# One moving operand of 512 columns for the gate and up products of the FFN, with the correction rows in the other half of the bank

## The reference, cut to what matters

```python
def _conv_ffn(x, w_up, conv_w, conv_b, w_down):      # x (1,256,1024), w_up (1024, 2*2816), w_down (2816,1024)
    u = _causal_dwconv(x @ w_up, conv_w, conv_b)     # 3 taps along the tokens, per feature
    gate, up = jnp.split(u, 2, axis=-1)
    return (jax.nn.silu(gate) * up) @ w_down
```

## Time and profile before

| | us |
|---|---|
| median of 3 runs (lowest, highest) | 829.93 (829.03, 830.1) |
| profiled execution, its own time | 828.89 |
| its span in the profile | 827.1 |
| PE busy in the span | 767.7 (93%) |
| DVE busy | 487.9 (59%) |
| ACT busy | 376.3 (45%) |

### The profile page before, as it was taken

How to read it: one execution, slowest core, us unless ns; L and a number is a source line. 1 busy time by engine, 2 the same in 40 slices (tenths; PEclk the granted TensorE clock), 3 DMA queues, 4 the chain that set the end, 5 groups by cost and what they waited for, 6 DMA issues and landing times.

```text
span 827.1 us, 16238 instructions
## 1 busy us (share of the span) xinstructions
PE 767.7 (93%) x6690; PEld 647.9 (78%) x6690; DVE 487.9 (59%) x843; ACT 376.3 (45%) x573; POOL 49.2 (6%) x91
## 2 busy tenths in 40 slices
PE   6999999999999999999999999999999877677676
PEld 6999998999999998999998999899955443344343
DVE  4455567767676678867864255487775523323326
ACT  4556664545545556567454553474332211111124
POOL 0200032000000000110101000000001000000000
PEclk9999999999999999999999999999999979879889
DMA  8964453556556554444342233449989999999993
GB/s 281 315 210 131 145 162 106 181 175 203 167 188 202 172 185 153 160 147 154 102 154 59 98 103 103 146 159 367 420 327 419 421 421 419 422 420 421 421 420 138
DMA packets 89170, 194.34 MB, mean 235 GB/s; under 512 B 3646, under 2 KB 69537, under 8 KB 76689
## 3 DMA queue, kind: packets, MB, share of 16 engines
q1 hardware_dynamic: 86640, 186.66, 61.3%
q0 software_dynamic: 1888, 4.61, 1.8%
q10 hardware_dynamic: 576, 2.14, 0.7%
HBM read 192.35 MB, written 1.05 MB: 234 GB/s over the span
## 4 chain that ended last, share of the span: by engine, by line
PE 72%; DMA 17%; DVE 5%; ACT 2%; issue 1%; SPq 1%; ACTq 0%; DVEq 0%
DMA expert_w<-in_expert_w_up 17%; PE PG L2041 15%; PE PG L2043 14%; PE PG L2042 14%; PE PG L2646 3%; PE PM L2041 3%; PE PM L2043 3%; PE PM L2042 3%; PE PM L2676 1%; PE PM L2497 1%; ACT whi L844 1%; PE PG L2668 1%; SPq L676 1%; PE PM L2122 1%; DMA rows<-in_norm_mix 1%
## 5 line engine op out<-in xcount | busy, mean ns | idle before, releaser
L2041 PE MATMUL PG<-hT_hi,whi 128*128 128x256 f32 (+1 forms) x816 | 235.8, 289 | 0.0
L2043 PE MATMUL PG<-hT_hi,wlo 128*128 128x256 f32 (+1 forms) x816 | 230.6, 283 | 0.0
L2042 PE MATMUL PG<-hT_lo,whi 128*128 128x256 f32 (+1 forms) x816 | 230.5, 282 | 0.0
L1357 DVE TENSOR_TENSOR wlo<-raw,whi 128x2048 fp32r<-128x2048 f32 x73 | 167.2, 2291 | 65.8 <-ACT whi L844 65.7
L2041 PEld LDWEIGHTS PG<-hT_hi,whi 128*128 128x128 f32 x816 | 153.9, 189 | 6.1 <-issue 2.8
L2043 PEld LDWEIGHTS PG<-hT_hi,wlo 128*128 128x128 f32 x816 | 154.2, 189 | 0.0
L2042 PEld LDWEIGHTS PG<-hT_lo,whi 128*128 128x128 f32 x816 | 153.7, 188 | 0.2
L844 ACT ACTIVATE whi<-raw 128x2048 fp32r<-128x2048 f32 x73 | 139.4, 1910 | 21.4 <-PE PG L2043 19.1
L2646 PE MATMUL PG<-expert_w,xw 128*32 128x256 f32 x992 | 74.2, 449 | 36.8 <-DMA expert_w<-in_expert_w_up 36.8
L2646 PEld LDWEIGHTS PG<-expert_w,xw 128*32 128x32 f32 x992 | 36.7, 124 | 59.0 <-issue 47.3
L1952 DVE SCALAR_TENSOR_TENSOR y_lo<-PG,small,y_hi 128x512 fp32r<-128x512 f32 x16 | 12.0, 750 | 98.4 <-ACT y_hi L1276 98.4
(11 more groups left out here) (525 smaller groups left out, 1338.3 us busy)
## 6 DMA issues: line engine op xcount, KB each, us to landing
expert_w<-in_expert_w_gate SPq DMA_DIRECT2D x32, 1024.0 KB, 26.7
expert_w<-in_expert_w_up SPq DMA_DIRECT2D x32, 1024.0 KB, 26.8
expert_w<-in_expert_w_down SPq DMA_DIRECT2D x32, 1024.0 KB, 26.9
raw<-in_ffn_w_up SPq DMA_DIRECT2D x22, 1024.0 KB, 5.0
raw<-in_w_in SPq DMA_DIRECT2D x22, 1024.0 KB, 5.1
raw<-in_moba_w_qkv SPq DMA_DIRECT2D x12, 1024.0 KB, 6.9
raw<-in_ffn_w_down SPq DMA_DIRECT2D x11, 1024.0 KB, 4.9
raw<-in_moba_w_o SPq DMA_DIRECT2D x4, 1024.0 KB, 5.1
```

Source lines behind the costliest of these rows:

```text
L1357: dve.tensor_tensor(lo_of(n), raw[:, n % R, :], hi_of(n).bitcast(F32), ALU.subtract).then_inc(s_lo, 1)
L2041: pe.matmul(dst, lh, rh, start=start, stop=False, **kw)
L2042: pe.matmul(dst, lh, rl, start=False, stop=False, **kw)
L2043: return pe.matmul(dst, ll, rh, start=False, stop=stop, **kw)
```

## The change

The activations' hi and lo parts become the two halves of one tile `hT`, so that one matmul can stream 256 columns of hi and 256 columns of lo as one moving operand of 512 columns against the hi weights. Its result fills a whole PG bank: hi·hi in the first half, hi·lo in the second. The lo weights times the hi activations are added to the second half, the correction. A new function `halves` issues these two matmuls for every k-tile in the place of the three of `split3`, in the FFN's gate and up granules only. Both halves have to be added afterwards: ACT copies the correction half of two banks to SBUF (`correction`), DVE adds the first half to it (the new function `halves` of the vector program) into `gate_sum` and `up_sum`, and `affine` and `taps` read these sums. PE waits for the adds instead of the taps. The issue order of ACT and DVE changes as the diff shows.

```diff
-        hT_hi = place("hT_hi", [P, KD, NT], 29440, F32R)
-        hT_lo = place("hT_lo", [P, KD, NT], 38144, F32R)
+        hT = place("hT", [P, 2, KD, NT], 29440, F32R)
+        hT_hi, hT_lo = (hT[:, i, :, :] for i in range(2))
+        gate_sum, up_sum = (place(n, [P, 2, SEQ], PH + 98304 + 2048 * i) for i, n in enumerate(("gate_sum", "up_sum")))
@@ scalar
-            def affine(j, dst, bank, tile0, s_done, par, cnt, gran):
-                act.wait_ge(s_gran, gran)
+            def correction(n, j, dst, bank, s_done, it):
+                act.wait_ge(s_gran, n + 1 + 6 * it)
+                act.activation(dst[:, :, :], PG[:, bank:bank + 2, SEQ:2 * SEQ], ACT.Copy).then_inc(s_done, 1)
+
+            def affine(j, dst, src, tile0, s_sum, s_done, par):
+                act.wait_ge(s_sum, 4 * j + 1)
                 for f in range(2):
-                    act.activation(dst[:, par, f, :], PG[:, bank + f, 0:SEQ], ACT.Identity,
+                    act.activation(dst[:, par, f, :], src[:, f, :], ACT.Identity,
             def ffn_step(n, j, par, it, first=False, last=False):
-                affine(j, cgate, 0, 2 * j, s_gaff, par, None, n + 1 + 6 * it)
+                correction(n, j, gate_sum, 0, s_gaff, it)
                 hi_part(n + 2, it)
-                act.wait_ge(s_gtap, 3 * j + 3)
+                affine(j, cgate, gate_sum, 2 * j, s_gtap, s_gaff, par)
+                correction(n + 1, j, up_sum, 2, s_uaff, it)
+                hi_part(n + 3, it)
+                act.wait_ge(s_gtap, 4 * j + 4)
                 act.activation(cgate[:, par, :, :], cgate[:, par, :, :], ACT.Silu).then_inc(s_gsilu, 1)
-                if last:
-                    hi_part(n + 3, it)
-                affine(j, cup, 2, FT + 2 * j, s_uaff, par, None, n + 2 + 6 * it)
-                if not last:
-                    hi_part(n + 3, it)
-                else:
+                affine(j, cup, up_sum, FT + 2 * j, s_utap, s_uaff, par)
+                if not first:
                     hi_part(n + 4, it)
                 act.wait_ge(s_hid, j + 1)
                 act.activation(hid_hi[:, par, :, :], hid[:, par, :, :], ACT.Copy).then_inc(s_hidhi, 1)
-                if not first and not last:
-                    hi_part(n + 4, it)
@@ vector (taps reads src = gate_sum or up_sum; its waits count 3 and 4 per step)
+            def halves(j, dst, bank, s_aff, s_tap):
+                dve.wait_ge(s_aff, 3 * j + 1)
+                dve.tensor_tensor(dst[:, :, :], PG[:, bank:bank + 2, 0:SEQ], dst[:, :, :], ALU.add).then_inc(s_tap, 1)
             def ffn_step(n, j, par, it, first=False, last=False):
-                taps(cgate, par, 0, 2 * j, s_gaff, s_gtap, j)
+                halves(j, gate_sum, 0, s_gaff, s_gtap)
                 lo_part(n + 2, it)
-                if last:
-                    lo_part(n + 3, it)
-                taps(cup, par, 2, FT + 2 * j, s_uaff, s_utap, j)
-                if not last:
-                    lo_part(n + 3, it)
+                taps(cgate, gate_sum, par, 2 * j, s_gaff, s_gtap, j)
+                halves(j, up_sum, 2, s_uaff, s_utap)
+                lo_part(n + 3, it)
+                taps(cup, up_sum, par, FT + 2 * j, s_uaff, s_utap, j)
                 dve.wait_ge(s_gsilu, j + 1)
-                dve.wait_ge(s_utap, 3 * j + 3)
+                dve.wait_ge(s_utap, 4 * j + 4)
                 dve.tensor_tensor(hid[:, par, :, :], cgate[:, par, :, :], cup[:, par, :, :], ALU.mult).then_inc(s_hid, 1)
+                if not first:
+                    lo_part(n + 4, it)
                 dve.wait_ge(s_hidhi, j + 1)
                 dve.tensor_tensor(hid_lo[:, par, :, :], ...).then_inc(s_hidlo, 1)
-                if not first:
-                    lo_part(n + 4, it)
@@ tensor
+            def halves(n, bank, it=0, ready=None):
+                pe.wait_ge(s_lo, n + 1 + 6 * it)
+                hw, lw = w_of(n)
+                for f in range(2):
+                    for k in range(KD):
+                        if ready is not None and f == 0 and k % 4 == 0:
+                            pe.wait_ge(ready[0], ready[1 + k // 4])
+                        x = slice(P * f, P * f + P)
+                        pe.matmul(PG[:, bank + f, :].rearrange("p (i n) -> p i n", i=2), hw[:, k, x], hT[:, :, k, 0:SEQ],
+                                  start=k == 0, stop=False, skip_group_check=True)
+                        mm = pe.matmul(PG[:, bank + f, SEQ:2 * SEQ], lw[:, k, x], hT[:, 0, k, 0:SEQ], start=False, stop=k == KD - 1,
+                                       skip_group_check=True)
+                mm.then_inc(s_gran, 1)
             def ffn_step(n, j, par, it, first=False):
-                    pe.wait_ge(s_gtap, 3 * j)
+                    pe.wait_ge(s_gtap, 4 * j - 3)
-                features(n, 0, hT_hi, hT_lo, slice(0, SEQ), it, halves=(s_xlo, 7, 8) if first else None)
+                halves(n, 0, it, (s_xlo, 7, 8) if first else None)
-                    pe.wait_ge(s_utap, 3 * j)
-                features(n + 1, 2, hT_hi, hT_lo, slice(0, SEQ), it)
+                    pe.wait_ge(s_utap, 4 * j - 3)
+                halves(n + 1, 2, it)
```

More of the change, by code:

```diff
@@ L1466, in col, with taps @@
                 return cols[:, bass.ds(i, n)]
-            def taps(dst, par, bank, tile0, s_aff, s_tap, j):
+            def halves(j, dst, bank, s_aff, s_tap):
+                dve.wait_ge(s_aff, 3 * j + 1)
+                dve.tensor_tensor(dst[:, :, :], PG[:, bank:bank + 2, 0:SEQ], dst[:, :, :], ALU.add).then_inc(s_tap, 1)
+            def taps(dst, src, par, tile0, s_aff, s_tap, j):
                 for back in (1, 2):
@@ L1472, in taps @@
                         if back == 1:
-                            dve.wait_ge(s_aff, 2 * j + f + 1)
+                            dve.wait_ge(s_aff, 3 * j + f + 2)
                         elif f == 0:
-                            dve.wait_ge(s_tap, 3 * j + 2)
-                        ins = dve.scalar_tensor_tensor(dst[:, par, f, back:SEQ], PG[:, bank + f, 0:SEQ - back],
+                            dve.wait_ge(s_tap, 4 * j + 3)
+                        ins = dve.scalar_tensor_tensor(dst[:, par, f, back:SEQ], src[:, f, 0:SEQ - back],
                                                        col((2 - back) * 2 * FT + tile0 + f), dst[:, par, f, back:SEQ],
@@ L2046, in w_of, with features @@
                 return (w.rearrange("p (k n) -> p k n", k=k) for w in (hi_of(n), lo_of(n)))
-            def features(n, bank, ah, al, c, it=0, halves=None, tiles=(0, 1), k0=0, k1=KD):
-                pe.wait_ge(s_lo, n + 1 + 6 * it)
+            def features(n, bank, ah, al, c, tiles=(0, 1), k0=0, k1=KD):
+                pe.wait_ge(s_lo, n + 1)
                 hw, lw = w_of(n)
@@ L2053, in features @@
                     for k in range(k0, k1):
-                        if halves is not None and f == 0 and k % 4 == 0:
-                            pe.wait_ge(halves[0], halves[1 + k // 4])
                         mm = split3(PG[:, bank + f, 0:c.stop - c.start], hw[:, k, P * f:P * f + P], lw[:, k, P * f:P * f + P],
```

## The result

The changed kernel takes 835.06 us (median of 4, 834.42 to 836.0) where the kernel before takes 830.01 beside it. The ratio is 1.0060 with a 95% interval of 1.0047 to 1.0074: 5.0 us slower, inside the range, with the forecast at 833.1. Its profiled execution took 834.42 us, with a span of 832.7.

A forecast was written before the change was run, and what follows sets the result against it. PE was taken to bound the FFN (busy 184.53 of 185.00 us), weight conversion just behind. Terms -3.55 - 1.4 + 1.5 + 4.5 gave +1.1, the clock's 2.1 made +3.2: from 829.93 to 833.1 us, range 829.0 to 836.8.

The forecast's parts named there:

- 352 pairs: FFN gate and up granules: each tile and k-tile pair falls from 0.3549 to 0.3448 us, 3.55 us less in all.
- hesitation in the steps: Steady FFN steps: PE's 0.15 us stall at the gate granule goes in each of nine steps, 1.4 us gained.
- first down product: Step 0's end: PE stalls 1.8 us instead of 0.34 before step 1's down product, 1.5 us lost.
- last down product: FFN's last step: conversions ahead of `hid_lo` make PE stall 5.0 us instead of 0.44, 4.5 us lost.
- lower clock: Last down product: the 5.0 us stall brings the granted clock to 0.50, 1.5 to 2.7 us lost, 2.1 taken.
- rival B: Last down product: the stall comes but the clock holds, 831.0 us; chance 0.18.
- Rival C: Gate and up pairs: fewer weight loads bring a pair near 0.325 us, total 826.2 us; chance 0.13.
- Rival D: Gate and up pairs: the wide operand's two pieces cost a second start, 836.6 us, or 839.6; chance 0.14.
- E: Last step: a conversion is ready earlier, the wait is 3 us less and the clock holds, 828.0 us; chance 0.07.
- A: The forecast itself: both late ends and the lower clock, 833.1 us, 831.5 to 835.5 within bounds; chance 0.48.

The follow-up runs named there:

- e4: Changed kernel with the 512-column matmul of hi weights split again into two of 256 columns, all else the same; 836.67 us, ratio 1.0078.
- e3: Changed kernel with ACT loading SiLU's table ahead of step 0's gate instead of in the middle of step 0; 834.21 us, ratio 1.0054.
- e7: Changed kernel with the first down product's weights converted already in step 0 and skipped in step 1; 832.76 us, ratio 1.0028.
- e8: Changed kernel, last step: last down product's weights converted ahead of the gate work, DVE's conversion for the next stage behind `hid_lo`; 830.0 us, ratio 1.0003.
- e1: Changed kernel, last step: DVE converts the last down product's lo weights between `hid` and `hid_lo`, the next stage's after `hid_lo`; 833.49 us, ratio 1.0042.
- e6: Changed kernel with 20 `keep_warm` calls (40 matmuls, 4.4 us) filling PE's wait ahead of the last down product; 833.23 us, ratio 1.0035.
- e5: Changed kernel with `hT` laid out so the moving operand's two pieces lie 1088 bytes apart instead of 8704; 835.59 us, ratio 1.0057.

## Why the prediction was right

Its sum put together losses and gains of five kinds; all of them were where it said, and the runs bear out the mechanism. The sum came out 1.6 us short at the FFN's end, 4.8 us late against 3.2 forecast, and 2.0 short in the median. The measured terms are from the traces of the two kernels:

| term | forecast, us | measured, us | from |
|---|---|---|---|
| 352 pairs | -3.55 | -2.3 | 352 x (0.3549 - 0.3484) |
| hesitation in the steps | -1.4 | -1.2 | gate granules of steps 2 to 10: 135.94 - 133.06 - 8 x 32 x 0.0065 |
| first down product | +1.5 | +1.6 | stall 1.91 against 0.34 |
| last down product | +4.5 | +4.4 | stall 4.81 against 0.44 |
| lower clock | +2.1 | +2.3 | 7.68 against 5.35 |
| sum | +3.2 | +4.8 | 4.8 seen |

- **The matmuls** are the mis-sized term. The price of the 512-column matmul was taken from the down product, 0.2265 us; with this operand it is 0.2306. The 1.3 us missing are most of the 1.6 by which the sum was short. e4 shows the saving itself.
- **The steady steps** went as forecast: the correction before `hi_part` lets the conversion end earlier than the affine did, and PE's small waits went. e4, with three matmuls and the new order, shows the gain by itself, 0.16 us a step. DVE, at 76% of the window, did not become the bound.
- **Step 0** had the right size by a partly wrong account, and that is luck. The forecast counted the table load of 1.28 us as the path to the up taps, 4.75 us after ACT's sight of up. DVE's conversion of the same step, which it left out, ends 4.73 us after it, so the time was the same either way; e3 shows that the load was worth 0.3 us. e7 shows that the place in the queue was the cause.
- **The last step** was read correctly from the order of the two lists. e8 shows it: another order of the same work takes away all but 1.4 us of the stall, and with it the lower clock, together some 5 us. One reading in it was wrong: before the change DVE's conversion was not done when the up affine came, and the taps waited for it:

```profile
309.69 2.29 DVE L1357 TENSOR_TENSOR own_lo<-raw,own_hi 128x2048 fp32r<-128x2048 f32 x1
311.90 1.77 DVE L1476 SCALAR_TENSOR_TENSOR cup<-PG,cols,cup 128x255 f32<-128x255 f32 x4
```

The sum was not hurt, since it took the end of `hid_lo` from the row. Counted from ACT's sight of up, the taps start 1.7 us on before and 4.65 after, which is 2.9 of the 4.4 us; `hid_lo` follows `hid` after 1.4 us before and 2.8 after, which is the other 1.4, the conversion for the next stage. e1 adds that ACT's conversion ahead of the affine holds the end up even where DVE's is out of the way.

- **The clock** fell as rival B said it would not. e6 shows its share without touching the stall. The stretch at 0.50 was 6.8 us long in this trace and 3.4 in e1's and e4's, with the product at 7.68 and 6.96 us; over all traces with a wait of 3.7 us or more there it took 6.89 (e3) to 8.25 us (e5). So the term moves between executions by more than 1 us, and that 2.1 met 2.3 is partly luck.
- Rival C (a pair of 0.325) was wrong. Rival D was right in kind and not in size: the wide matmul is dearer than the down product's, but at 0.2306 us, not 0.2366 and above, so that the pair, 0.3484, lies between the forecast's 0.3448 and D's 0.3549. E was wrong: nothing was ready earlier.

The distance between 4.8 us at the FFN's end and 5.0 in the medians is within what the medians can tell. The range, 829.0 to 836.8, also holds rival B's 831.0 and rival D's 836.6, so the total alone would not have told A from them; the terms above do.

## What to carry to other kernels

A saving in the engine that bounds the middle of a loop can be smaller than what a changed order does to the loop's first and last pass (here 3.5 us gained against 8.3 lost): count those two passes by themselves, instruction by instruction, for every helper engine. Work for the next stage belongs behind the last value that the bounding engine waits for: here it cost 1.4 us by the rows, though no run moves it alone. A wait of several microseconds in front of dense matmuls costs its length and, by the granted clock, a part of the following work once more; filling it with idle matmuls bought 2.1 us back here, taking most of it away some 5.

## What the runs showed of the hardware

- A matmul on 512 columns of `hT` in two pieces costs 0.2306 us (0.2322 with the pieces near each other), one on 512 columns of weights in one piece 0.2265, two of 256 columns 0.237. That the pieces are the reason is not shown. Fewer, wider matmuls save here 6.5 ns for each matmul that goes, not 10.
- PE waits of 1.4 to 1.9 us kept the granted clock at 1.00 (1.4 at e8's last product, 1.9 at the changed kernel's first one); behind 3.7 us in e1 and 4.8 us in the changed kernel it was 0.50.
- A `keep_warm` call on fp32 constants is recorded as two matmuls of 0.111 us each at 128 columns.
- ACT's copy of 512 elements from PSUM took 0.598 us and DVE's add 0.69, near the 0.582 and 0.686 of the earlier trace rows; an affine pair of 256 elements each took 1.08 us from SBUF and 1.02 from PSUM.
